# Decode attention whose score and value products go through 32-column groups of the array

## The reference, cut to what matters

```
s_past = einsum('bqhd,bkhd->bhqk', q, k_past) * scale
s_new  = einsum('bqhd,bkhd->bhqk', q, k) * scale      # causal inside the 4 new tokens
p = softmax(concat([s_past, s_new]))                  # per sub-head
a = p[:, :, 0] - lam * p[:, :, 1]                     # per head, two sub-heads each
out = einsum('bhqk,bkhe->bqhe', a, v)                 # per head, 128 wide
```

## Time and profile before

| | before |
|---|---|
| median of three runs | 1547.0 us |
| lowest, highest | 1543.46, 1553.66 us |
| span of the profiled execution | 1539.1 us |
| TensorE multiplying | 1306.9 us (85%) |
| TensorE loading weights | 883.9 us (57%) |
| VectorE, ScalarE, GpSimd | 744.7, 568.3, 283.7 us |
| mean granted clock of TensorE | 0.937 |

### The profile page before, as it was taken

One profiled execution on the slowest core, in us unless ns is written; L12 is line 12 of the kernel. 1 busy time (PEld: TensorE's weight loads), 2 busy tenths in 40 slices (PEclk: granted clock), 3 DMA queues, 4 the chain that ended last, 5 costly groups with the idle time before them and its releaser, 6 DMA issues.

```text
span 1539.1 us, 20098 instructions
## 1 busy us (share of the span) xinstructions
PE 1306.9 (85%) x5769; PEld 883.9 (57%) x5770; DVE 744.7 (48%) x1101; ACT 568.3 (37%) x786; POOL 283.7 (18%) x289
## 2 busy tenths in 40 slices
PE   4879999999997799789999899638989989899920
PEld 1334444366665466566565688426767777677720
DVE  4863232201113887511011454567865556888747
ACT  4530111000001556422232122206755546777633
POOL 0020000010000111000000011112554344554424
PEclk9989999999998999999999899758999999999965
DMA  8981200011100200077664311406875765888545
GB/s 288 367 318 32 82 28 26 16 46 42 41 0 0 84 1 1 1 233 237 193 173 126 127 41 42 183 16 247 303 269 200 272 251 218 313 303 324 216 157 184
DMA packets 84544, 230.86 MB, mean 150 GB/s; under 512 B 16101, under 2 KB 28517, under 8 KB 72165
## 3 DMA queue, kind: packets, MB, share of 16 engines
q1 hardware_dynamic: 70288, 203.80, 37.6%
q0 software_dynamic: 14192, 26.24, 4.8%
HBM read 220.42 MB, written 34.21 MB: 165 GB/s over the span
## 4 chain that ended last, share of the span: by engine, by line
PE 64%; DVE 10%; DMA 9%; issue 7%; ACT 5%; POOL 2%; DVEq 2%; ACTq 1%; SPq 1%; POOLq 0%
PE psum L530 19%; PE psum L583 12%; PE psum L611 11%; PE psum L690 4%; DMA xg<-h_scratch,gidx 4%; PE psum L517 4%; PE psum L705 2%; PE psum L629 2%; DMA wada<-in_w_ada_dram 2%; PE psum L638 2%; DVE xgL L1493 1%; ACT pexp L922 1%; DVEq L332 1%; PE psum L672 1%; DMA wgu<-in_w_up_dram 1%
## 5 line engine op out<-in xcount | busy, mean ns | idle before, releaser
L583 PE MATMUL psum<-wqkv,hT 128*128 128x512 f32 (+1 forms) x432 | 187.5, 594 | 0.0
L611 PE MATMUL psum<-hT,wcv 128*128 128x352 f32 x576 | 170.9, 459 | 0.0
L1485 DVE TENSOR_TENSOR wguL<-wgu,wguH 128x2048 fp32r<-128x2048 f32 x64 | 146.7, 2294 | 39.9 <-ACT wguH L1034 39.2
L530 PE MATMUL psum<-wguH,xgH 128*128 128x512 f32 x320 | 130.8, 409 | 33.0 <-DVE xgL L1493 33.0
L611 PEld LDWEIGHTS psum<-hT,wcv 128*128 128x128 f32 x576 | 109.3, 190 | 60.6
L583 PEld LDWEIGHTS psum<-wqkv,hT 128*128 128x128 f32 (+1 forms) x432 | 77.8, 182 | 103.2 <-issue 103.1
L1034 ACT CAST wguH<-wgu 128x2048 fp32r<-128x2048 f32 x64 | 120.3, 1912 | 23.5 <-issue 14.2
L530 PE MATMUL psum<-wguH,xgL 128*128 128x512 f32 x320 | 126.7, 396 | 0.0
L530 PE MATMUL psum<-wguL,xgH 128*128 128x512 f32 x320 | 126.4, 395 | 0.0
L1553 POOL TENSOR_SCALAR small<-small 128x1 f32<-128x1 f32 (+3 forms) x36 | 20.1, 559 | 508.4 <-ACT ajunk L1011 213.5
L629 PE MATMUL psum<-kT,qz 128*128 128x512 f32 (+3 forms) x192 | 77.7, 520 | 19.5 <-ACT pexp L922 18.2
(11 more groups left out here) (269 smaller groups left out, 2412.1 us busy)
## 6 DMA issues: line engine op xcount, KB each, us to landing
wgu<-in_w_gate_dram SPq DMA_DIRECT2D x32, 1024.0 KB, 4.9
wgu<-in_w_up_dram SPq DMA_DIRECT2D x32, 1024.0 KB, 7.5
wdn<-in_w_down_dram SPq DMA_DIRECT2D x32, 1024.0 KB, 7.4
wada<-in_w_ada_dram SPq DMA_DIRECT2D x24, 1024.0 KB, 8.2
kseq<-in_cache_k_dram SPq DMA_DIRECT2D x64, 256.0 KB, 3.0
vseq<-in_cache_v_dram SPq DMA_DIRECT2D x64, 256.0 KB
yg<-y_scratch SPq DMA_DIRECT2D x16, 512.0 KB, 4.9
wqkv<-in_w_in_dram SPq DMA_DIRECT2D x1, 6144.0 KB, 25.3
```

What stands on the lines that cost most here:

```text
L530: ins = mm(out, r32(x(c)), r32(w(c)), start=(begin and c == 0 and k == 0), stop=(end and c == chunks - 1 and k == 2))
L583: last = mm(psum[0:n, 2 + j, :], hT[:, c, P * t:P * t + n], wqkv[:, c, AW * j:AW * j + AW], start=(c == 0), stop=(c == DC - 1))
L611: last = mm(psum[:, 3 * (n % 2) + j, 0:TB], wcv[i % 2][:, c, j, :], hT[:, c, TB * tb:TB * tb + TB], start=(c == 0), stop=(c == DC - 1))
L1485: TT(r32(wguL[slot][:, g, :, :]), wgu[slot][:, g, :, :], wguH[slot][:, g, :, :], ALU.subtract).then_inc(S["wguL_done"], 1)
```

## The change

The four chunks of a page's scores no longer accumulate. Chunk c goes into the 32 PSUM partitions 32c to 32c+31, which are the array's columns 32c to 32c+31, each as a product of its own. The same holds for the new keys. In each chunk the queries now stand in columns 0 to 7 (`a = 4 * u`), so the rows 32c to 32c+7 are used and the others are zero products. Everything between, the maxima, the exponentials, the sums, `pdec`, `snew`, `pairs` and the constant tables, has 128 rows instead of 32. L684 therefore contracts over 128 rows, with a `pairs` matrix of 128x16 in which the unused rows are zero.

The value products are split by heads: in place of one product of 128 columns of `aTs` with 512 value columns there are four of 32 columns with the head's own 128 value columns, into the partitions 32h to 32h+31 and columns 0 to 127 of bank 6. The number of L517 products stays the same; the value products go from 9 to 36 for each sequence. Semaphores, buffers and the order of the work are not changed.

```
--- before.py
+++ after.py
@@ -81,12 +81,13 @@
     rows_of = 1 + tok[:, :, None] + TOK * np.arange(2)
     put("tokid", np.where(ok[:, :, None], rows_of, 0).astype(np.float32))
     put("valid", ok.astype(np.float32))
-    r = np.arange(SUBS * LNEW)
+    h, r = i // NSAMP, i % NSAMP
     put("dmask", np.where(np.arange(LNEW)[None, :] <= (r % LNEW)[:, None], 0.0, NEG).astype(np.float32))
     cols = np.arange(HEADS * LNEW)
-    put("pair", ((r // (2 * LNEW))[:, None] * LNEW + (r % LNEW)[:, None] == cols[None, :]).astype(np.float32))
-    put("sub0", ((r // LNEW) % 2 == 0).astype(np.float32)[:, None])
-    put("sub1", ((r // LNEW) % 2 == 1).astype(np.float32)[:, None])
+    mine = (h * LNEW + r % LNEW)[:, None] == cols[None, :]
+    put("pair", (mine & (r < 2 * LNEW)[:, None]).astype(np.float32))
+    put("sub0", (r // LNEW == 0).astype(np.float32)[:, None])
+    put("sub1", (r // LNEW == 1).astype(np.float32)[:, None])
     put("tilecol", i[:, None].astype(np.float32))
     put("half", np.full((P, 1), -0.5, np.float32))
     return c
@@ -193,11 +194,11 @@
         vnew = [at("vnew0", O_W + 28 * K + 512, [LNEW, AW]), at("vnew1", O_X + 32 * K, [LNEW, AW])]
         qbd = at("qbd", O_W + 24 * K, [P, NSEQ, 4, 32])
         kTp = [at(f"kTp{i}", O_H + 24 * K + 2 * K * i, [P, 4, P]) for i in range(2)]
-        pdec = [at(f"pdec{i}", O_H + 4 * K * i + 512 * i, [32, PAGES * P + LNEW]) for i in range(2)]
+        pdec = [at(f"pdec{i}", O_H + 4 * K * i + 512 * i, [P, PAGES * P + LNEW]) for i in range(2)]
 
         aTs = [at(f"aTs{i}", O_H + 9 * K + 5 * K * i, [P, PAGES + 1, P]) for i in range(2)]
-        snew = [at(f"snew{i}", O_H + 19 * K + 64 * i, [32, LNEW]) for i in range(2)]
-        pairs = [at(f"pairs{i}", O_H + 19 * K + 128 + 64 * i, [32, 16]) for i in range(2)]
+        snew = [at(f"snew{i}", O_H + 19 * K + 64 * i, [P, LNEW]) for i in range(2)]
+        pairs = [at(f"pairs{i}", O_H + 19 * K + 128 + 64 * i, [P, 16]) for i in range(2)]
         orow = at("orow", O_X + 32 * K, [NSAMP, HEADS, P])
         pt_sb = at("pt_sb", O_W + 28 * K, [1, NSEQ * PAGES], I32)
 
@@ -258,8 +259,8 @@
         r1s = [small[:, 32:36], small[:, 89:93]]
         hss, hrs, hsc = small[:, 36:40], small[:, 40:44], small[:, 44:48]
         lsum = small[:, 48:52]
-        dmx, dl, dr = small[0:32, 52:57], small[0:32, 57:60], small[0:32, 60:64]
-        sgn = small[0:32, 64:65]
+        dmx, dl, dr = small[:, 52:57], small[:, 57:60], small[:, 60:64]
+        sgn = small[:, 64:65]
         ss2, rs2 = small[:, 66:75], small[:, 75:84]
 
 
@@ -514,8 +515,8 @@
             if p == 0 and s >= 2:
                 pe.wait_ge(W["dexp_done"], 2 * s - 2)
             for c in range(4):
-                last = nc.tensor.matmul(psum[0:32, 2 * (s % 2) + p // 4, P * (p % 4):P * (p % 4) + P], qbd[:, s, c, :], kTp[n % 2][:, c, :],
-                                        start=(c == 0), stop=(c == 3))
+                last = nc.tensor.matmul(psum[32 * c:32 * c + 32, 2 * (s % 2) + p // 4, P * (p % 4):P * (p % 4) + P], qbd[:, s, c, :],
+                                        kTp[n % 2][:, c, :], start=True, stop=True)
             last.then_inc(S["dscore_ps"], 1)
 
         @block.tensor
@@ -686,10 +687,12 @@
                 pe.wait_ge(W["da_sb"], s + 1)
                 pe.wait_ge(W[f"vseq_in{s % 2}"], 16 * (PAGES + 1) * (s // 2 + 1))
                 for p in range(PAGES + 1):
-                    if p < PAGES:
-                        last = mm(psum[:, 6, :], aTs[s % 2][:, p, :], vseq[s % 2][:, p, :], start=(s == 0 and p == 0), stop=False)
-                    else:
-                        last = mm(psum[:, 6, :], aTs[s % 2][0:LNEW, p, :], vnew[s % 2][:, :], start=False, stop=(s == NSEQ - 1))
+                    for h in range(HEADS):
+                        own, cols = slice(32 * h, 32 * h + 32), slice(P * h, P * h + P)
+                        if p < PAGES:
+                            last = mm(psum[own, 6, 0:P], aTs[s % 2][:, p, own], vseq[s % 2][:, p, cols], start=(s == 0 and p == 0), stop=False)
+                        else:
+                            last = mm(psum[own, 6, 0:P], aTs[s % 2][0:LNEW, p, own], vnew[s % 2][:, cols], start=False, stop=(s == NSEQ - 1))
                 last.then_inc(S["do_ps"], 1)
 
             pe.wait_ge(W["qbd_done"], 1)
@@ -710,7 +713,7 @@
                 if s >= 2:
                     pe.wait_ge(W["da_sb"], s - 1)
                 for c in range(4):
-                    last = mm(psum[0:32, 7, 256:256 + LNEW], qbd[:, s, c, :], kTs[:, c, LNEW * s:LNEW * s + LNEW], start=(c == 0), stop=(c == 3))
+                    last = mm(psum[32 * c:32 * c + 32, 7, 256:256 + LNEW], qbd[:, s, c, :], kTs[:, c, LNEW * s:LNEW * s + LNEW], start=True, stop=True)
                 last.then_inc(S["ds_ps"], 1)
                 if s >= 1:
                     sample_values(s - 1)
@@ -968,7 +971,7 @@
                 if s >= 2:
                     act.wait_ge(W["da_ps"], s - 1)
                 b, m = s % 2, dmx[:, 3 + s % 2:4 + s % 2]
-                A(pdec[b][:, 0:PAGES * P], psum[0:32, 2 * b:2 * b + 2, :].rearrange("p b n -> p (b n)"), ACT.Exp, bias=m,
+                A(pdec[b][:, 0:PAGES * P], psum[:, 2 * b:2 * b + 2, :].rearrange("p b n -> p (b n)"), ACT.Exp, bias=m,
                   accum_out=dl[:, 0:1]).then_inc(S["dexp_done"], 1)
                 A(pdec[b][:, PAGES * P:], snew[b][:, :], ACT.Exp, bias=m, accum_out=dl[:, 1:2]).then_inc(S["dexp_done"], 1)
                 if s in (4, 5, 6):
@@ -1003,7 +1006,7 @@
             lead_of_mix(1)
 
             for h in range(HEADS):
-                nc.scalar.copy(orow[:, h, :], psum[32 * h:32 * h + 32, 6, P * h:P * h + P]).then_inc(S["oT_sb"], 1)
+                nc.scalar.copy(orow[:, h, :], psum[32 * h:32 * h + 32, 6, 0:P]).then_inc(S["oT_sb"], 1)
             act.wait_ge(W["oT_sb"], 4)
             for h in range(HEADS):
                 if h:
@@ -1136,7 +1139,7 @@
             link(TS(neglam, neglam, -LAM_INIT, None, ALU.add))
             link(TS(gsub, gsub, 1.0 - LAM_INIT, None, ALU.mult))
             dve.wait_ge(W["const_in"], 16)
-            link(STT(sgn, C("sub1", 32), neglam[0:32, :], C("sub0", 32), ALU.mult, ALU.add))
+            link(STT(sgn, C("sub1"), neglam, C("sub0"), ALU.mult, ALU.add))
             for b in range(ADAB):
                 if b + 1 < ADAB:
                     rest_of_ada(2 * b + 2)
@@ -1275,7 +1278,7 @@
                     for c in range(4):
                         for u in range(2):
                             r = slice(64 * u, 64 * u + 64)
-                            a = 8 * c + 4 * u
+                            a = 4 * u
                             last = nc.vector.tensor_copy(qbd[r, :, c, a:a + LNEW], qTs[r, c, :].rearrange("p (s q) -> p s q", s=NSEQ))
                     last.then_inc(S["qbd_done"], 1)
                 if h == 2 and i >= 1:
@@ -1286,9 +1289,9 @@
             def sample_maxima(s):
                 b = s % 2
                 dve.wait_ge(W["ds_ps"], s + 1)
-                TT(snew[b][:, :], psum[0:32, 7, 256:256 + LNEW], C("dmask", 32), ALU.add).then_inc(S["dnew_done"], 1)
+                TT(snew[b][:, :], psum[:, 7, 256:256 + LNEW], C("dmask"), ALU.add).then_inc(S["dnew_done"], 1)
                 dve.wait_ge(W["dnew_done"], s + 1)
-                RED(dmx[:, 0:1], psum[0:32, 2 * b:2 * b + 2, :].rearrange("p b n -> p (b n)"), AX_X, ALU.max)
+                RED(dmx[:, 0:1], psum[:, 2 * b:2 * b + 2, :].rearrange("p b n -> p (b n)"), AX_X, ALU.max)
                 link(RED(dmx[:, 1:2], snew[b][:, :], AX_X, ALU.max))
                 link(TT(dmx[:, 2:3], dmx[:, 0:1], dmx[:, 1:2], ALU.max))
                 TS(dmx[:, 3 + b:4 + b], dmx[:, 2:3], -1.0, None, ALU.mult).then_inc(S["dmax_done"], 1)
@@ -1309,7 +1312,7 @@
                 link(TT(dl[:, 2:3], dl[:, 0:1], dl[:, 1:2], ALU.add))
                 link(nc.vector.reciprocal(dr[:, 0:1], dl[:, 2:3]))
                 link(TT(dr[:, 1:2], dr[:, 0:1], sgn, ALU.mult))
-                TS(pairs[s % 2][:, :], C("pair", 32), dr[:, 1:2], None, ALU.mult).then_inc(S["pair_done"], 1)
+                TS(pairs[s % 2][:, :], C("pair"), dr[:, 1:2], None, ALU.mult).then_inc(S["pair_done"], 1)
 
             dve.wait_ge(W["attT_ps"], 8)
             for b in range(2):
```

23 lines of the change are left out of this document (12 added, 11 removed).

## The result

The changed kernel takes 1499.24 us in the median (1495.69 to 1507.86, 4 runs) against 1545.23 (the three runs above and a fourth): ratio 0.9707, 95% interval 0.9651 to 0.9763, 46 us less. The forecast was 1516 with a range of 1500 to 1550; the median lies just under it. The direction was right, the size was not: the gain is one and a half times the one worked out.

A forecast was written before the change was run, and what follows sets the result against it. TensorE was taken to bound the decode part. The terms -15.2 - 21.2 + 4.3 + 1.2 = -30.9 us took the median from 1547.0 to 1516, with an 8-in-10 range of 1500 to 1550.

The forecast's parts named there:

- The overlap: TensorE's neighbouring matmuls in different column groups: only the hand-over d shrinks, from 0.11 to 0.031 us, at best 0.
- steps 1 and 2: Scores: three shorter hand-overs a page, -15.2 us over 64 pages; values: 0.294 us less a block, -21.2 over 72.
- A: No overlap between column groups, each next group starting 0.11 us later; time 1549 us; chance 0.14.
- B: Each change of column group drains the array, 0.11 us a change; time 1600 us; chance 0.12.
- C: Overlap in scores only (1533 us) or values only (1527 us); chance 0.08, of it 0.05 for values alone.
- Step 5: SyncE's page loads: 18.3 us a sequence keeps up with 20.9, except one new wait for sequence 3's keys, +4.3.
- D: Page loads set the pace, 19.6 us a sequence, at no extra cost: 1516 us; chance inside the forecast's 0.66.
- Step 3: Operations going from 32 to 128 partitions (maximum, exp, weight loads of L684) keep their time: 0 us.
- Step 4: ScalarE's 0.585 us copy of transposed keys stays covered beside TensorE: 0 us; uncovered up to 37.
- Step 6: Tail: VectorE's low parts of the output weights, then mixL, hold back the first mixing products: +1.2 us.
- Step 7: Loads of x after the last values move along with them, so the gain is carried to the end.
- The clock: TensorE's half-speed stretches stay in every sequence; the new wait may add one, at most +1.7 us, kept for the range.

The follow-up runs named there:

- the order experiments: The changed kernel with its score or value products reordered, four kernels: 1517.44, 1500.03, 1506.42 and 1501.38 us.
- group_major: Changed kernel, each chunk's scores as two consecutive 64-key products, values head by head with new-key products between heads: 1517.44 us, ratio 0.9811.
- pool_spread: Changed kernel with value loads issued by GpSimd instead of SyncE and the output-weight load cut into four parts: 1472.19 us, ratio 0.9534.

## Why the prediction was right and wrong

**The overlap** failed, and with it the sizes of steps 1 and 2. The prediction said: "The two records of one matmul share a group, so they stay 0.11 apart; and starts are in order. Hence only the hand-over from one matmul to the next can shrink". The first half held: the second four records of a page start 0.13 us after the first four. The second, "starts are in order", had no row behind it, since no row of before has two matmuls in different groups, and the order experiments show it false. The records of one matmul are serial only inside their own group, and the other groups don't wait for them. So a page's scores shrank by 0.63 us and not by 0.237, and the value block at full clock from 6.9 to 1.88 us, not to about 4.5. Even its most hopeful price, d = 0, gave 1507 and not 1499. The rule of the Trainium skill that I set against it (TensorE: Matmul & The Clock Gate, Part 3: tiles about 4 ns apart) was the better guide for the distance; this case measures 0.007 us. I had put its 4 ns only into the hand-over and kept my order of starts around it. Its table of speed-ups, 2.38 for three column tiles, is also of the kind seen here: 3.7 for four.

**Rivals.** A and B are out. A change of column group costs 0.007 us and not 0.11. A change of shape does cost: 0.20 us from record to record at the new-key products of group_major instead of 0.109, and the heads on both sides don't overlap. This is the rule of the Trainium skill that I had set against B (TensorEngine Tiling (Array Packing), Key Properties); the changed kernel agrees with its half on tiles, group_major with its half on modes. C is out, both places overlap.

**Step 5, SyncE's queue**, had the right pace (18.3 us; 18.65 measured) but set it against a sequence of 20.9 us that followed from the wrong overlap. TensorE's own sequence is 15 to 16 (15.1 to 16.3 in pool_spread). The prediction wrote of the queue that "it keeps up, except once"; in fact TensorE waited for keys at each of the sequences 3 to 7. The wait before sequence 3 was 15.6 us and not 4.3: the keys came when the prediction had them (708.85; 709.4), but TensorE wanted them at 693.2 and not at 705.1. D named this and priced it at nothing; it said itself that this held only for the larger d. The cause was tested: the same move of the value loads gives 24 us in the changed kernel and none before.

**Why the miss is only 17 us.** Two errors cancelled in part, and that is luck. By TensorE's own terms the change is worth 64 x 0.63 = 40 us in the scores and about 5.6 us in each of eight value blocks (9.56 us from L690 to the next transposes, 3.5 to 4.2 now), 45: together 85. The decode part became 43 us shorter (the last new-value products begin at 810.2 instead of 853.6). Of the 42 that are missing most is SyncE's: with both reliefs the decode part is 128.8 us and before it was 205.1, so 76 of the 85 are there, 33 more than in the changed kernel. The last 9 I can't separate; the clock is the likely taker.

**Step 3**: right; maxima and exponentials of 128 rows cost what those of 32 did (the maximum 1.224 us in the mean against 1.212, the exponential 1.114 against 1.104; the earlier trace rows names shapes up to 512 columns only, so the 1.23 for 1024 had been read across). **Step 4**: right for all pages but the last of a sequence, where 0.32 us of waiting for the copy appeared in every sequence, 2.6 us in all, under cover of SyncE. **Step 6**: right in kind. mixL started at 814.39, directly behind the 9.15 us of low parts, and the first product 5.0 us after the last new-value products began, where it was 2.6: +2.3 us and not +1.2. **Step 7**: right in kind. VectorE resumes at 830.68 instead of 871.60, 40.9 earlier. The spans differ by 45.3; the other 4.4 arise in the expert loop, where nothing changed: from the first to the last of its 40 tiles it took 417.8 us before and 412.9 after, and 413.0 to 416.7 in the other kernels whose value loads SyncE issues. I count it as spread, not as gain.

**The clock** I had kept for the range at 1.7 us. It fell much further, to 0.73 over the part. The sign that I had set for the scores, under 0.9, came up in one place: 1.00 in the stretch at 679.5, but 0.77 from 708.8 to 718.2, which began at 1.2 GHz after the wait of 15.6 us. Waiting for pages is not the whole cause: pool_spread has no such wait, its clock is 0.80, and its value blocks, which follow short gaps of 0.4 to 0.5 us around the products with `pairs`, still take 3.3 to 3.6 us instead of 1.9. What the fallen clock costs once SyncE is relieved was not measured.

## What to carry to other kernels

Narrow products in neighbouring column groups run side by side, even with fp32's two records, if the program goes round the groups. Two in a row for one group cost nothing here and eight did (a value block of 5.9 us instead of 1.9); a product of another shape between them kept the groups apart. Before costing a faster engine, write down the pace of every queue that feeds it, to the microsecond per iteration, and compare it with the new period under the best case as well as the likely one: here one queue, with its 18.3 us a sequence and one long stand, took 33 of the 85 us that TensorE had gained. When a small change uncovers a DMA-issuing engine, look for an idle engine's queue, and for small loads standing behind a big one, and look at the stages behind it too: here a part of the gain was lost again in the expert loop.

## What I had not expected of the hardware

- Four fp32 products of 32 columns and 128 streamed columns in four column groups take 0.36 us up to the next transposes; in one group they took 0.99.
- A product for a free column group starts before an earlier one that waits for a busy group (16 records in 0.39 us). With eight in a row for a group, two of them overlap with the next group.
- Two small loads issued behind a 4 MB load held their queue for 9.5 and 3.5 us; in front of it 0.6 and 1.5.
- The decode part's mean granted clock went from 0.93 to 0.73 in the changed kernel, and whole value blocks ran at 1.2 GHz; without any wait for pages it was 0.80, with the value blocks still at 1.2 GHz for most of their time.
